# The opening of a two-layer backbone on one core: tokens laid out by channel, squares added before they are summed, modulation of two tiles at a time

## The reference, cut to what matters

```python
mod_x = silu(c) @ ada_w[0] + ada_b[0]         # c: latent tokens; c_ctx: context tokens
sx1, cx1, gx1, sx2, cx2, gx2 = split(mod_x, 6)
hx = (x * rsqrt(mean(x * x, -1) + 1e-6) * norm1_g[0]) * (1 + cx1) + sx1
z  = hx @ pw1_w + pw1_b                       # (1024, 2048): a value and a gate half
u  = a * sigmoid(g)                           # then a convolution of 31 taps along the tokens
```

## Time and profile before

| | us |
|---|---|
| median of three runs (lowest, highest) | 1671.44 (1670.82, 1672.15) |
| the profiled execution | 1671.6 |
| its span, first to last instruction | 1669.7 |
| PE busy in the span | 1641.5 (98%) |
| DVE busy | 958.0 (57%) |
| ACT busy | 677.3 (41%) |
| POOL busy | 168.6 (10%) |
| DMA | 165.64 MB, mean 99 GB/s |

### The profile page before, as it was taken

How to read it: one execution, slowest core, us unless ns; L and a number is a source line. 1 busy time by engine, 2 the same in 40 slices (tenths; PEclk the granted TensorE clock), 3 DMA queues, 4 the chain that set the end, 5 groups by cost and what they waited for, 6 DMA issues and landing times.

```text
span 1669.7 us, 25661 instructions
## 1 busy us (share of the span) xinstructions
PE 1641.5 (98%) x10040; PEld 1435.3 (86%) x10040; DVE 958.0 (57%) x1511; ACT 677.3 (41%) x1019; POOL 168.6 (10%) x180
## 2 busy tenths in 40 slices
PE   6999989999999999999999999999999999999998
PEld 4777758998888888888899999999999888888888
DVE  6899987763424342334358665656566754543445
ACT  4656667542323222223245333424244543332333
POOL 1488851000000000000000000000000000000000
PEclk9999999999999999999999999999999999999999
DMA  9767742221221212121112121212112323232321
GB/s 338 254 251 251 252 160 95 75 76 48 67 76 56 70 60 67 55 71 57 57 51 92 64 70 39 83 51 63 58 64 76 99 81 123 89 101 89 100 88 51
DMA packets 58062, 165.64 MB, mean 99 GB/s; under 512 B 5288, under 2 KB 7192, under 8 KB 57976
## 3 DMA queue, kind: packets, MB, share of 16 engines
q1 hardware_dynamic: 54120, 150.43, 27.1%
q0 software_dynamic: 2992, 10.88, 2.0%
q10 hardware_dynamic: 864, 3.15, 0.5%
HBM read 162.34 MB, written 2.10 MB: 98 GB/s over the span
## 4 chain that ended last, share of the span: by engine, by line
PE 82%; DVE 14%; ACT 3%; issue 1%; DMA 0%; ACTq 0%; DVEq 0%
PE ps L674 81%; DVE ps L1867 3%; DVE ps L1884 3%; DVE w_lo L1663 2%; DVE rstd L1669 1%; DVE H_lo L1704 1%; PE ps L879 0%; DVE tmp L1692 0%; DVE ps L1882 0%; ACT sq L1251 0%; DVE sq L1692 0%; DVE rstd L1680 0%; ACT tmp L1251 0%; ACT H_hi L1242 0%; DVE ps L1864 0%
## 5 line engine op out<-in xcount | busy, mean ns | idle before, releaser
L674 PE MATMUL ps<-H_hi,w_hi 128*128 128x512 f32 (+1 forms) x1712 | 583.3, 341 | 8.4 <-DVE H_lo L1766 5.1
L674 PE MATMUL ps<-H_lo,w_hi 128*128 128x512 f32 (+1 forms) x1712 | 578.8, 338 | 0.0
L674 PE MATMUL ps<-H_hi,w_lo 128*128 128x512 f32 (+1 forms) x1712 | 578.1, 338 | 0.0
L674 PEld LDWEIGHTS ps<-H_hi,w_hi 128*128 128x128 f32 x1712 | 324.7, 190 | 62.2 <-issue 24.4
L674 PEld LDWEIGHTS ps<-H_hi,w_lo 128*128 128x128 f32 x1712 | 324.8, 190 | 35.0
L674 PEld LDWEIGHTS ps<-H_lo,w_hi 128*128 128x128 f32 x1712 | 324.9, 190 | 34.3
L1663 DVE TENSOR_TENSOR w_lo<-w_raw,w_hi 128x1024 fp32r<-128x1024 f32 x208 | 255.0, 1238 | 107.9 <-ACT w_hi L1204 75.0
L674 PE MATMUL ps<-mid_hi,w_hi 128*128 128x512 f32 (+1 forms) x592 | 199.4, 337 | 0.6
L674 PE MATMUL ps<-mid_lo,w_hi 128*128 128x512 f32 (+1 forms) x592 | 198.4, 335 | 0.0
L674 PE MATMUL ps<-mid_hi,w_lo 128*128 128x512 f32 (+1 forms) x592 | 198.0, 335 | 0.0
L2200 DVE SCALAR_TENSOR_TENSOR tmp<-ps,par,tmp 128x511 f32<-128x511 f32 x66 | 41.6, 658 | 231.3 <-ACT tmp L1548 155.1
(11 more groups left out here) (278 smaller groups left out, 2097.0 us busy)
## 6 DMA issues: line engine op xcount, KB each, us to landing
w_raw<-in_w_units SPq DMA_DIRECT2D x190, 512.0 KB, 3.5
ada<-in_ada_w SPq DMA_DIRECT2D x40, 1024.0 KB, 6.4
w_raw<-in_w_units SPq DMA_DIRECT2D x16, 384.0 KB, 3.3
ada<-in_ada_w POOLq DMA_DIRECT2D x4, 1024.0 KB, 13.1
conv<-in_x ACTq DMA_DIRECT2D x4, 512.0 KB, 5.6
ada_more<-in_ada_w POOLq DMA_DIRECT2D x2, 1024.0 KB, 14.6
conv<-in_ctx ACTq DMA_DIRECT2D x2, 512.0 KB, 9.4
w_raw<-in_w_units POOLq DMA_DIRECT2D x2, 512.0 KB, 18.5
```

Of the source, the lines that this page charges most:

```text
L674: return nc.tensor.matmul(o, a, b, start=first, stop=last, skip_group_check=True)
```

## The change

The host now hands over the tokens by channel (`x_cols`), the parameters as one table of columns (`params`), and the modulation weights so that each half group is 8 KB in a row per partition (`ada_groups`). Of layer 0 the first 2048 modulation columns are reordered: group m holds the shift of tiles 2m and 2m+1 and then their scale. Token transposes, parameter transposes and the batch statistics are gone. ACT squares the eight tiles of `X`, DVE adds the squares of the eight tiles up, and six one-column products sum each token over the partitions. Then root, reciprocal, diagonals and the two spreading products as before, now ahead of `ada_products(0)`. Modulation, shifting and the k-steps go in groups of two tiles. POOL waits for half of the tokens. The diff, cut to its core:

```diff
-FIRST_GROUPS = [0, 2, 1, 3]
+FIRST_GROUPS = 4
...
+        def x_square(k):
+            return conv[:, k, 0:TOK] if k < KT - 1 else norm_buf[0]
...
+            sp.dma_start(par[:], params).then_inc(par_in, 16)
+            for n in range(KT // 2):
+                sp.dma_start(X[:, 2 * n:2 * n + 2, :], x_cols[:, 2 * n:2 * n + 2, :]).then_inc(x_in[n], 16)
+            sp.dma_start(ident[:], eye).then_inc(eye_in, 16)
...
-            pool.wait_ge(tokens_in[0], 32)
+            pool.wait_ge(x_in[1], 16)
             def load_gate_or_value(unit):
                 pool.dma_start(w_raw[:, unit, :], w_units[unit]).then_inc(first_raw[unit], 16)
@@ -598,10 +579,9 @@
             for m in range(2):
                 for half in range(2):
                     load_first(pool, m, half)
-            load_gate_or_value(0)
+                load_gate_or_value(m)
             for half in range(2):
                 load_first(pool, 2, half)
-            load_gate_or_value(1)
             for half in range(2):
                 pool.wait_ge(ada_done, 1 + half)
                 load_first(pool, 3, half)
...
-            pe.wait_ge(eye_in, 16)
-            token_transposes(0)
-            token_transposes(1)
-            def par_transposes(blocks, bank):
-                for n, (j, rows) in enumerate(blocks):
-                    m = nc.tensor.transpose(ps[:, bank, n * P:n * P + rows], prow[0:rows, j, :], ident[0:rows, 0:rows])
-                m.then_inc(par_T, 1)
-            pe.wait_ge(par_rows, 16 * 12)
-            par_transposes([(0, 128), (1, 116)], 6)
-            token_transposes(2)
-            pe.wait_ge(silu_c_ready, 2)
-            pe.wait_ge(par_ready, 1)
-            ada_products(0)
-            pe.wait_ge(tap_rows, 16 * 4)
-            par_transposes([(2, 128), (3, 120), (4, 66), (5, 66)], 1)
-            ada_transposes(0)
-            pe.wait_ge(filled, 4)
+            pe.wait_ge(filled, 1)
+            pe.wait_ge(x_added, KT - 1)
+            for t in range(6):
+                m = mm(tok_sums[:, t:t + 1], x_squares[:, t * P:(t + 1) * P], mean_of[:, 0:1], True, True)
+            m.then_inc(x_summed, 1)
             pe.wait_ge(diag_ready, 1)
-            pe.wait_ge(slot_read[1], S_PW1 // 2)
             mm(ps[:, 3, :], mean_of[:], flat_sq[:, LATS], True, True)
             mm(ps[:, 4, 0:CTX], mean_of[:], flat_sq[:, CTXS], True, True).then_inc(rows_ready, 1)
-            ada_products(1)
-            ada_transposes(1)
+            pe.wait_ge(silu_c_ready, 2)
+            ada_products(0)
+            pe.wait_ge(eye_in, 16)
+            ada_transposes(0)
             def first_block(h, k0, k1):
@@ -912,22 +868,22 @@
                 unit_product(h, h, KT, (H_hi, H_lo), streams, (h0_lo_ready, 0), unit_done if k1 == KT else None, k0, k1,
                              value_lat_done if h and k1 == KT else None)
-            for p in range(2):
-                pe.wait_ge(slot_read[p], S_PW1 // 2)
-            first_block(0, 0, 1)
+            ada_products(1)
+            ada_transposes(1)
+            first_block(0, 0, 2)
             ada_products(2)
-            first_block(0, 1, 3)
+            first_block(1, 0, 2)
             ada_transposes(2)
-            first_block(0, 3, 4)
-            pe.wait_ge(par_ready, 2)
+            first_block(0, 2, 4)
             ada_products(3)
-            first_block(1, 0, 1)
+            first_block(1, 2, 3)
             ada_transposes(3)
-            first_block(1, 1, 4)
-            first_block(0, KT // 2, KT - 2)
+            first_block(1, 3, 4)
+            first_block(0, 4, 6)
+            first_block(1, 4, 6)
+            first_block(0, 6, KT)
             ada_products(4)
-            first_block(0, KT - 2, KT)
-            first_block(1, KT // 2, KT)
+            first_block(1, 6, KT)
             ada_transposes(4)
             ada_products(5)
...
-            for s in range(S_PW1):
-                t, jj = s // 4, s % 4
-                if s == 8:
-                    act.wait_ge(par_ready, 1)
-                    for v in range(2):
-                        A(silu_c[:, :, v], par[:, C_COL + 8 * v:C_COL + 8 * v + 8], ACT.Silu).then_inc(silu_c_ready, 1)
-                act.wait_ge(xT_done, s + 1)
-                A(X[:, 2 * jj:2 * jj + 2, part(t)], bank(s % 2, 0).rearrange("p (a n) -> p a n", a=2), ACT.Copy) \
-                    .then_inc(slot_read[s % 2], 1)
-            act.wait_ge(tok_var, 2)
-            A(tok_rstd[:], tok_mv[:, :, 1], ACT.Sqrt, bias=eps[:, 0:1]).then_inc(tok_std, 1)
-            ada_copy(0)
-            ada_copy(1)
-            split_hi(0, 0)
+            act.wait_ge(par_in, 16)
+            for v in range(2):
+                A(silu_c[:, :, v], par[:, C_COL + 8 * v:C_COL + 8 * v + 8], ACT.Silu).then_inc(silu_c_ready, 1)
+            for k in range(KT):
+                act.wait_ge(x_in[k // 2], 16)
+                A(x_square(k), X[:, k, :], ACT.Square).then_inc(x_squared, 1)
+            A(tok_std_row, eps[:, 0:1], ACT.Sqrt)
+            act.wait_ge(x_summed, 1)
+            A(tok_rstd[:], tok_sums, ACT.Sqrt, bias=eps[:, 0:1]).then_inc(tok_std, 1)
             def first_hi(j):
-                act.wait_ge(mod_ready, 2 if j < KT // 2 else 4)
+                act.wait_ge(mod_ready, 2 * (j // 2) + 2)
                 act.wait_ge(xn_ready, j + 1)
                 for m, toks in groups(True):
                     a = A(H_hi[:, j, toks], xn(j, toks), ACT.Identity, scale=gain[:, 0, 0, j, m:m + 1],
-                          bias=mod[:, 0, j, m:m + 1])
+                          bias=mod[:, 0, first_shift(j), m:m + 1])
                 a.then_inc(h0_hi_ready, 1)
-            for j in range(KT // 2):
-                first_hi(j)
-            split_hi(1, 1)
-            ada_copy(2)
-            ada_copy(3)
-            for j in range(KT // 2, KT):
-                first_hi(j)
-                if j in (4, 6):
-                    split_hi(j // 2, j // 2)
+            for m in range(FIRST_GROUPS):
+                if m < 2:
+                    split_hi(m, m)
+                ada_copy(m)
+                for j in (2 * m, 2 * m + 1):
+                    first_hi(j)
+            split_hi(2, 2)
+            split_hi(3, 3)
             ada_copy(4)
...
+            def first_modulation(m):
+                dve.wait_ge(mod_sum, m + 1)
+                js = slice(2 * m, 2 * m + 2)
                 rows = par[:, ADA_B:ADA_B + 2 * KT].rearrange("p (a j) -> p a j", a=2)[:, :, js]
-                cols = mod[:, 0, 0:2 * KT, :].rearrange("p (a j) c -> p a j c", a=2)[:, :, js, :]
-                v.tensor_tensor(cols, cols, rows.unsqueeze(3).to_broadcast([P, 2, GROUP, 2]), ALU.add).then_inc(mod_ready, 1)
-                dve.wait_ge(mod_ready, 2 * half + 1)
-                v.scalar_tensor_tensor(gain[:, 0, 0, js, :], mod[:, 0, KT + half * GROUP:KT + (half + 1) * GROUP, :], 1.0,
-                                       two(par[:, NORM1 + half * GROUP:NORM1 + (half + 1) * GROUP]), ALU.add, ALU.mult) \
+                cols = mod[:, 0, 4 * m:4 * m + 4, :].rearrange("p (a j) c -> p a j c", a=2)
+                v.tensor_tensor(cols, cols, rows.unsqueeze(3).to_broadcast([P, 2, 2, 2]), ALU.add).then_inc(mod_ready, 1)
+                dve.wait_ge(mod_ready, 2 * m + 1)
+                v.scalar_tensor_tensor(gain[:, 0, 0, js, :], mod[:, 0, 4 * m + 2:4 * m + 4, :], 1.0,
+                                       two(par[:, NORM1 + 2 * m:NORM1 + 2 * m + 2]), ALU.add, ALU.mult) \
                     .then_inc(mod_ready, 1)
-                dve.wait_ge(mod_ready, 2 * half + 2)
+                dve.wait_ge(mod_ready, 2 * m + 2)
...
-            for t in range(6):
-                if t % 2 == 0:
-                    dve.wait_ge(tokens_in[t // 2], 32)
-                if t == 4:
-                    dve.wait_ge(par_T, 1)
-                    v.tensor_copy(par[:, 0:244], ps[:, 6, 0:244]).then_inc(par_ready, 1)
-                for half in range(2):
-                    o = v.bn_stats(tok_st[:, t, half, :], xin[:, t, half * 512:(half + 1) * 512])
-            o.then_inc(tok_stats, 1)
-            dve.wait_ge(tok_stats, 1)
-            for t in range(6):
-                o = v.bn_aggr(tok_mv[:, t, :], tok_st[:, t, :, :])
-            o.then_inc(tok_stats, 1)
-            dve.wait_ge(tok_stats, 2)
-            v.tensor_tensor(tok_rstd[:], tok_mv[:, :, 0], tok_mv[:, :, 0], ALU.mult).then_inc(tok_var, 1)
-            dve.wait_ge(tok_var, 1)
-            v.tensor_tensor(tok_mv[:, :, 1], tok_mv[:, :, 1], tok_rstd[:], ALU.add).then_inc(tok_var, 1)
+            for k in range(1, KT):
+                dve.wait_ge(x_squared, k + 1)
+                if k > 1:
+                    dve.wait_ge(x_added, k - 1)
+                v.tensor_tensor(x_squares, x_square(0) if k == 1 else x_squares, x_square(k), ALU.add) \
+                    .then_inc(x_added, 1)
+            dve.wait_ge(par_in, 16)
             dve.wait_ge(tok_std, 1)
             v.reciprocal(tok_rstd[:], tok_rstd[:]).then_inc(tok_rstd_ready, 1)
```

(63 more changed lines are left out.)

88 lines of the change are left out of this document (28 added, 60 removed).

## The result

The changed kernel takes a median of 1675.99 us over 12 executions against 1671.27 (1670.33 to 1672.15, also 12) for the kernel before on the same chip: 4.7 us slower. One of its executions was in a slow state, 2020.38 us at a mean granted clock of 0.755; without it the median is 1675.84 (1673.41 to 1676.91), 4.6 us slower, ratio 1.0025, 95% interval 1.0018 to 1.0033. The prediction was 1670.8 with 1667.9 to 1674.2: the median lies outside. The eleven executions fall into two groups, 1673.4 to 1674.0 (four) and 1675.7 to 1676.9 (seven). The profiled one, 1673.41 with a span of 1671.6, is the fastest of all. It is compared first; the other group has a profile of its own in the last experiment.

What follows compares the result with a forecast made beforehand. DVE's taps bound the kernel from 58.85 to 214.7 us, so only the context multiply's start counted: 58.2, 0.6 us earlier. Profiled 1671.6 - 0.6 = 1671.0, or 1670.8 against the median; range 1667.9 to 1674.2.

Steps and rivals of the forecast that it cites:

- sums at 15.35: Opening: last add of squares done at 15.35, then six one-column products at the lower clock, 2.6 us, to 17.95.
- normalizing at 22.96: Opening, after root, diagonals and spreading products: normalizing was to start at 23.0, where the kernel before had 24.29.
- The last pair of tiles: Token load: the last pair was to land at 12.6 (bounds 11.6 and 13.6), with six tiles' squares hidden under it.
- ACT as the releaser of L1894: Before the taps: ACT's copy 4, table load and sigmoids, not PE, release DVE's latents multiply (L1969 before) at 57.2.
- The 1.00 in the clock column: Start of the profile: the recorded 1.00 is no measurement; TensorE starts at the lower level, 1.2 GHz.
- when does L1972 start in the changed kernel?: DVE's context multiply ahead of the taps (L1897 after the change): 58.2 instead of 58.85, 0.6 us earlier, the whole forecast.
- The tightest has 1 us, so I charge nothing: Weight loads, groups 0 to 3: land at 19.1, 26.0, 32.9, 38.3, before use, so no cost.
- Whatever moves the 58.85 moves all behind it by as much: DVE's taps to 214.7, DVE busy 151.83 of 153 us: a shift of the context multiply's start passes on undiminished.
- I let it rise at 24.5: TensorE's clock in products 0: rises at 24.5, so products 0 end at 25.7 (24.9 to 26.8).
- TensorE stays at 1.2 GHz: Rival, 20%: first four k-steps and products 2 run slow; context multiply at 61.3, 1673.9 us, up to 1677.8.
- the forecast of 1671.0: Main forecast, 42%: profiled execution 1671.6 less 0.6 us; 1669.5 to 1672.

Runs made afterwards that it cites:

- run 12: The last experiment: the changed kernel unaltered, one execution, for a profile of the slower group; 1676.48 us.
- run 4: Changed kernel with products 4 moved ahead of the gate unit's last two k-steps; 1672.55 us, +1.4 over the kernel before.
- run 5: Kernel before with only products 4 moved later, behind all of the gate unit and the value unit's k-steps 4 and 5; 1676.17 us, +5.3.
- run 10: Changed kernel with products 4 ahead of the gate's last two k-steps and of the value's k-step 5, no fillers; 1669.72 us, -1.2 against the kernel before.
- runs 9: Changed kernel with only ten fillers (throwaway matmuls) between products 1 and transposes 1, in the wait for row 1; 1673.07 us, +2.2 over the kernel before.
- 3: Changed kernel with fillers (throwaway matmuls) from the start, behind adds 1 to 6, and ten in the wait for row 1; 1673.37 us, +2.2.
- 11: Changed kernel with run 10's order, ten fillers in the wait for row 1, and fillers before the sums and in the diagonals' wait; 1670.00 us, -0.9.

## Why the prediction was wrong

**What held.** The paces and the first 23 us: sums at 15.35 (forecast 15.35) at the lower level in 2.69 (2.6), normalizing at 22.96 (23.0). That the sums agree to the hundredth is luck. The last pair of tiles was in at 11.89, not 12.6, and what came last was DVE's chain of adds, which follow each other by 1.04 where I had taken 0.96 and hidden six tiles under the load:

```profile
11.89 0.84 ACT L1227 ACTIVATE conv<-X 128x768 f32<-128x768 f32 x1 [0.36 <-DMA X<-in_x_cols]
```

```profile
8.93 5.21 DVE L1726 TENSOR_TENSOR conv<-conv 128x768 f32<-128x768 f32 x5 [0.25 <-ACT conv L1227]
```

Also right: ACT as the releaser of L1894, through copy, table load and sigmoids: 3.0 from copy 4 at 56.34 to L1894 at 59.34, where I had 2.9. Groups 0 to 3 of the weights cost nothing. The 1.00 in the clock column ahead of its first change was rightly not believed.

**The step that failed: "So the whole question is one number: when does L1972 start in the changed kernel?"**, with "Weights: ... The tightest has 1 us, so I charge nothing". I costed products 4 by what they take on TensorE and what comes behind them, and the weights only up to group 3. Their end also releases a buffer. Moved behind the whole gate unit, they issue the load for products 5 3.9 us later, and block 1 of the taps starts 1.55 later than block 0 alone explains (+2.98 against +1.43). Runs 4 and 5 show it from both sides and run 10 removes the wait. "Whatever moves the 58.85 moves all behind it by as much" was wrong twice: block 1 has a wait of its own, and behind 214 the clock of the execution decides 1.3 us. In the executions where the clock also falls behind these waits, the place of products 4 costs about 1.5 more. In run 12 block 1 starts 24.95 behind block 0, in the kernel before 21.83: 3.1 us, the largest part of the miss.

**A size that failed: the clock.** I let it rise at 24.5, inside products 0, and the first k-steps run at 2.4 GHz. In the profiled execution products 0 ended at 26.4, 0.7 behind the forecast, and the first k-steps were at the lower level. From there the whole row stands about 2 us late: products 4 at 54.35 (52.4), L1894 at 59.34 (57.2), L1897 at 60.28 (58.2). That is the rival "TensorE stays at 1.2 GHz", which I gave 20% and priced at 1673.9; the profiled execution had 1673.41. Fillers in the wait (runs 9 and 3) are worth 2.4 and 2.2. But that the price fits is luck: the rival put L1897 at 61.3 and it came at 60.28, and the rest is the wait for weights, which the rival didn't name.

**The median** lies 2.6 above the profiled execution. Run 12 (1676.48) shows how one such execution gets there from the forecast of 1671.0: 1.7 at block 0 (59.88 against 58.2), 3.1 between block 0 and block 1, and 0.8 behind the table load at 248.91 (1425.79 us to the end against 1424.97 before). Its fall at 220 us is no part of that, since the profile on which the forecast rests had the same. How far this holds for the whole group is open: there are three profiles of 23 executions. Why run 4 has no second group is not settled either; its products 5 wait once for 0.90 us and its clock holds there, as in all five profiles with products 4 early, which fits but wasn't tested by itself. Nor is it settled why the clock's rise in products 0 varies (3.54, 3.35, 2.75, 2.67, 2.10 us for the same sixteen matmuls).

The opening by channel itself does start the normalizing 1.3 us earlier than before (22.96 against 24.29), as forecast. With products 4 early (run 10) the kernel is 5.8 us better than as changed, and as fast as the kernel before within what is measured.

## What to carry to other kernels

When a block of work is moved, ask what its end releases. If it frees a buffer, cost the load that waits for that buffer and the place that needs it, one or two blocks further on than the step that the change is about. Each new wait of a microsecond or two at TensorE is also a chance for its clock to fall, so its price is the wait and sometimes the work behind it at half pace. Compare several executions before you read a few microseconds from one profile: a fall that one of two profiles has, as at 216 to 222 us here, looks like an effect of the change.

## What the runs showed of the hardware

The same wait ends in either clock. TensorE is idle about 2 us behind the last tap block, between 210 and 222 us. In the profiles of before and of runs 4, 11 and 12 the granted clock fell to 0.50 for some 3 us behind it, in the other ten it stayed at 1.00. From 20 to 35 us, when the modulation weights come in, the changed kernel's transfers ran at 419 to 424 GB/s with rows of 8 KB, the kernel before's at 383 to 392 with rows of 2 KB; no run changes the rows alone. And fillers can cost as much as they bring: 24 small matmuls (48 in the record) took 8.12 us at a mean granted clock of 0.68 and held up the sums that they were to speed.
